# Second block's mixer: splits of queries and keys and the spread of the mLSTM's maxima moved into the projection, gates in pieces, the mLSTM's end pulled apart

## The reference

```
def hybrid_mixer(h, w_in, gate_bias, g_q, g_k, g_mh, w_out):
    proj = (h @ w_in)                       # 1024 -> 3088 columns
    mq, mk, mv, mo, mg, aq, ak, av = split(proj)
    gates = mg.reshape(B, S, 4, 4).transpose(2, 0, 3, 1) + gate_bias
    hm = bidirectional_mlstm(mq, mk * 64 ** -0.5, mv,
             gates[0], log_sigmoid(gates[1]), gates[2], log_sigmoid(gates[3]))
    hm = rms_norm(hm, g_mh) * sigmoid(mo)                  # 4 heads of 128
    qa = partial_rope(rms_norm(aq, g_q), pos) * 64 ** -0.5 # 8 heads of 64
    ka = partial_rope(rms_norm(ak, g_k), pos)
    ha = dilated_attention(qa, ka, av)      # windows 128, 512, 2048; dilations 1, 4, 16
    return concatenate([hm, ha]) @ w_out

mlstm, one direction, per head:  b = cumsum(log_f);  m_t = running maximum
    s = exp(b_t - b_s + li_s - m_t) * (q_t . k_s)  for s <= t
    h = (s @ v) / max(|sum_s s|, exp(-m_t))
```

## Time and profile before

| | us |
|---|---|
| median of three runs | 3399.1 |
| the profiled execution's own time | 3399.85 |
| its span on the core | 3397.7 |
| PE busy in the span | 3129.7 (92%) |
| DVE busy | 1918.7 (56%) |
| ACT busy | 1025.8 (30%) |
| mean granted TensorE clock | 0.947 of full |
| stage of the change: projection, first matmul | 2596.13 |
| side by side, first matmul | 2775.28 |
| output projection, first matmul | 2960.96 |

### The profile page before, as it was taken

The page is one execution under the profiler, slowest core; times in us unless marked ns, Lnnn a source line. Parts: engine busy times, 40 slices in busy tenths (PEclk is TensorE's granted clock), DMA queues, the critical chain, the costliest instruction groups (busy, mean ns, idle before and its releaser), DMA issues.

```text
span 3397.7 us, 36171 instructions
## 1 busy us (share of the span) xinstructions
PE 3129.7 (92%) x14590; PEld 2494.5 (73%) x14590; DVE 1918.7 (56%) x2716; ACT 1025.8 (30%) x1472; POOL 30.3 (1%) x32
## 2 busy tenths in 40 slices
PE   4999999898889999899978999899997989799998
PEld 3788888786667888788865788678886754377886
DVE  6876555635555544566656554566665555554344
ACT  2322222335443222322222222332224245332222
POOL 2000000000000000000000000000000000000000
PEclk6999999898989999999988999899998989699999
DMA  5443333110023433256521443235552200122221
GB/s 189 130 136 131 112 112 106 48 62 10 2 93 127 171 126 109 95 172 216 179 95 61 144 155 124 75 113 192 185 173 70 82 33 1 42 90 98 99 93 51
DMA packets 101905, 365.33 MB, mean 108 GB/s; under 512 B 11230, under 2 KB 12526, under 8 KB 101484
## 3 DMA queue, kind: packets, MB, share of 16 engines
q1 hardware_dynamic: 97644, 351.65, 30.8%
q10 hardware_dynamic: 2944, 6.29, 0.5%
q0 software_dynamic: 1152, 5.07, 0.5%
HBM read 360.87 MB, written 2.10 MB: 107 GB/s over the span
## 4 chain that ended last, share of the span: by engine, by line
PE 84%; DVE 10%; ACT 4%; issue 1%; DMA 1%; ACTq 0%; DVEq 0%; SPq 0%
PE ps L191 24%; PE ps L193 23%; PE ps L192 23%; PE ps L195 4%; PE ps L196 2%; DVE WL L183 1%; DVE DUMP L304 1%; DMA STG<-in_w_modt 1%; ACT WH L178 1%; PE ps L507 1%; DVE RAW L1301 1%; PE ps L2607 0%; DVE XT L815 0%; DVE SQ L575 0%; PE ps L483 0%
## 5 line engine op out<-in xcount | busy, mean ns | idle before, releaser
L191 PE MATMUL ps<-HH,WH 128*128 128x512 f32 x2464 | 980.4, 398 | 34.2 <-DVE HL L564 27.9
L192 PE MATMUL ps<-HL,WH 128*128 128x512 f32 x2464 | 969.3, 393 | 0.0
L193 PE MATMUL ps<-HH,WL 128*128 128x512 f32 x2464 | 968.9, 393 | 0.0
L178 ACT ACTIVATE WH<-RAW 128x1024 fp32r<-128x1024 f32 x456 | 456.6, 1047 | 554.8 <-PE ps L193 409.4
L183 DVE TENSOR_TENSOR WL<-RAW,WH 128x1024 fp32r<-128x1024 f32 x456 | 538.4, 1220 | 103.6 <-ACT WH L178 103.4
L191 PEld LDWEIGHTS ps<-HH,WH 128*128 128x128 f32 x2464 | 468.7, 190 | 144.6 <-issue 42.2
L192 PEld LDWEIGHTS ps<-HL,WH 128*128 128x128 f32 x2464 | 468.6, 190 | 100.2 <-issue 3.8
L193 PEld LDWEIGHTS ps<-HH,WL 128*128 128x128 f32 x2464 | 468.0, 190 | 101.0
L815 DVE SCALAR_TENSOR_TENSOR XT<-ps,DER,XT 128x512 f32<-128x512 f32 x512 | 342.7, 682 | 272.7 <-PE ps L193 258.1
L191 PE MATMUL ps<-GH,WH 128*128 128x512 f32 x1056 | 414.5, 392 | 19.1 <-DVE XT L815 14.3
L192 PE MATMUL ps<-GL,WH 128*128 128x512 f32 x1056 | 412.1, 390 | 0.0
(11 more groups left out here) (358 smaller groups left out, 2409.7 us busy)
## 6 DMA issues: line engine op xcount, KB each, us to landing
RAW<-in_w_modt SPq DMA_DIRECT2D x200, 512.0 KB, 4.5
RAW<-in_ffn_wi SPq DMA_DIRECT2D x176, 512.0 KB, 4.5
RAW<-in_ffn_wo SPq DMA_DIRECT2D x88, 512.0 KB, 4.8
RAW<-in_w_gu SPq DMA_DIRECT2D x88, 512.0 KB, 4.4
RAW<-in_w_in SPq DMA_DIRECT2D x44, 512.0 KB, 3.7
RAW<-in_w_down SPq DMA_DIRECT2D x44, 512.0 KB, 4.5
RAW<-in_w_out SPq DMA_DIRECT2D x16, 512.0 KB, 4.8
MU<-in_w_mod SPq DMA_DIRECT2D x8, 384.0 KB, 8.0
```

Source lines behind the costliest of these rows:

```text
L178: act.e.activation(u.hi, u.ld.view, ACT.Copy).then_inc(u.hi_done.sem, 1)
L191: pe.e.matmul(out, wh, x[0], start=first, stop=False)
L192: pe.e.matmul(out, wh, x[1], start=False, stop=False)
L193: m = pe.e.matmul(out, wl, x[0], start=False, stop=last)
```

## The change

It does the following.

- The ring of weights shrinks from five places to three ahead of the projection (`Ring.shrink`), and the two freed places hold MB, now written during the projection; NUM and MD take the three kept places later. The RAW slots for weights go from six to two ahead of the projection, not behind it, since QH and KH lie in the other four.
- The splits of the attention's queries and keys become a fourth piece behind the rope (`normed_rope`) in the projection. `Begin` waits for the last one.
- `MlTables` moves from `mlstm` into the projection, to where MG is evacuated; SELF, SEL, MKD and other small tiles share memory. The gates' evacuation is two ACT copies of 36 rows instead of four of 4 (columns of the weights and of the bias are put in another order). `MlScan` becomes `MlCum` (cumulative sums), `MlMax` (maxima) and `MlFloor` (the exponential, first thing in `mlstm`).
- `MlBroadcast` is made for one head and direction, eight pieces in the projection, one per chunk, over a side bank (there are four side banks now, 4 to 7, for three).
- The order of chunks is another one: DQ and DV first, MG third, DK and MV taking turns, the four MO last.
- `mlstm`'s pieces: a unit pair (two of the 16 units) takes three pieces instead of four; behind `MlDen` there are three rounds; each `MlSquare` comes two pieces behind its `MlQuot`; behind `MlNewton` there are four rounds. `extra=4` is gone.

```
-                    self.add(MlScan(m))
+                    self.add(MlCum(m))
                     yield
+                    self.add(MlMax(m))
                     yield
                     self.add(MlTurnU(m, pr))
+                    m.mgsplit = self.add(HiLo(self, m.MG, m.MGH[:, :], m.MGL[:, :], [m.max]))
+                    for h in range(4):
+                        for d in range(2):
+                            yield
+                            self.add(MlBroadcast(m, pr, h, d))
...
-                rest = list(range(DV, NIN2)) + list(range(MQ, MG))
-                order = [MG]
-                for i in range(8):
-                    order += [DQ + i] + rest[2 * i:2 * i + 2]
+                order = [DQ, DV, MG, DV + 1, DQ + 1, DV + 2, DV + 3, DQ + 2, MQ, MQ + 1, DQ + 3, MK, MK + 1]
+                for i in range(4):
+                    order += [DK + i, MV + i]
+                order += list(range(MO, MG))
...
-            self.add(Begin([self.group, self.roped, self.turned, self.evacd] + lent))
+            self.add(Begin([self.group, self.turned, self.evacd, ksplit[3].done]))
...
-            self.side_by_side(self.dilated(w, CF, cf, DQt, DKt), self.mlstm(m, mix, a["w_out_2"]), extra=4)
+            self.side_by_side(self.dilated(w, CF, cf), self.mlstm(m, mix, a["w_out_2"]))
...
-        for h in range(4):
-            self.add(MlBroadcast(m, h))
-            yield
         before = None
         for h in range(4):
             self.add(MlMask(m, h))
             for j in range(4):
                 x = self.add(MlExp(m, h, j))
-                yield
+                if j % 2:
+                    yield
                 if before:
                     self.add(MlSum(m, before))
                 self.add(MlProd(m, x))
                 before = x
                 yield
         last = self.add(MlSum(m, before))
-        yield
         self.add(MlDen(m, last.done))
         m.rsplit = self.add(HiLo(self, m.B, m.RH[:, :], m.RL[:, :], [m.inverse]))
-        yield
-        yield
+        for _ in range(3):
+            yield
+        before = None
         for h in range(4):
             quot = self.add(MlQuot(m, h))
             yield
-            self.add(MlSquare(m, h, quot))
+            if before:
+                self.add(MlSquare(m, h - 1, before))
+            before = quot
+            yield
+        self.add(MlSquare(m, 3, before))
         self.add(MlNewton(m))
```

More of the change, by code:

```diff
@@ L145, in __init__ @@
     def __init__(self, P, ld, ring):
-        n = ring.n
+        at = ring.places[ring.n % len(ring.places)]
         ring.n += 1
-        at = n % ring.size
         self.ld = ld
@@ L157, with __init__, shrink @@
 class Ring:
-    def __init__(self, WH, WL, size):
-        self.WH, self.WL, self.size, self.n, self.at = WH, WL, size, 0, {}
+    def __init__(self, WH, WL, places):
+        self.WH, self.WL, self.places, self.n, self.at = WH, WL, list(places), 0, {}
+    def shrink(self, n):
+        size = len(self.places)
+        order = [self.places[(self.n - 2 + i) % size] for i in range(size)]
+        self.places, self.n = order[:n], 2
+        return order[n:], [self.at[at].used for at in order[n:]]
 class Split(Step):
@@ L2094, in scalar @@
         m, t = self.m, self.t
+        act.wait_ge(*m.sel)
         act.wait_ge(*self.ready)
@@ L2100, in scalar, with direction @@
         act.e.activation(m.EM, m.EM, ACT.Ln, bias=1.0).then_inc(t[2].sem, 1)
-class MlScan(Step):
+def direction(x, d):
+    x = x[32 * d:32 * d + 4, :]
+    return x if d == 0 else x[:, ::-1]
+class MlCum(Step):
     def __init__(self, m):
         self.m = m
-        self.t = [m.P.s["ml_dve"].next() for _ in range(7)]
-        self.em = m.P.s["ml_act"].next()
-        m.scan = self
-    @staticmethod
-    def rows(x, d):
-        x = x[32 * d:32 * d + 4, :]
-        return x if d == 0 else x[:, ::-1]
+        self.t = [m.P.s["ml_dve"].next() for _ in range(4)]
+        m.u = self.t[3]
     def vector(self, dve):
-        m, t, rows = self.m, self.t, self.rows
+        m, t = self.m, self.t
         dve.wait_ge(*m.gates)
@@ L2128, in vector, with __init__ @@
         dve.e.tensor_tensor(m.U, m.U, m.B, ALU.subtract).then_inc(t[3].sem, 1)
-        dve.wait_ge(*t[3])
-        for d in range(2):
-            u = rows(m.U, d)
-            dve.e.tensor_tensor_scan(rows(m.MG, d), u, u, -BIG, ALU.max, ALU.max).then_inc(t[4 + d].sem, 1)
-        dve.wait_ge(*t[5])
-        dve.e.tensor_tensor(m.EM, m.B, m.MG, ALU.add).then_inc(t[6].sem, 1)
+class MlMax(Step):
+    def __init__(self, m):
+        self.m = m
+        self.t = [m.P.s["ml_dve"].next() for _ in range(3)]
+        m.max = self.t[2]
+    def vector(self, dve):
+        m, t = self.m, self.t
+        dve.wait_ge(*m.u)
+        for d in range(2):
+            u = direction(m.U, d)
+            dve.e.tensor_tensor_scan(direction(m.MG, d), u, u, -BIG, ALU.max, ALU.max).then_inc(t[d].sem, 1)
+        dve.wait_ge(*t[1])
+        dve.e.tensor_tensor(m.EM, m.B, m.MG, ALU.add).then_inc(t[2].sem, 1)
+class MlFloor(Step):
+    def __init__(self, m):
+        self.m = m
+        m.em = m.P.s["ml_act"].next()
     def scalar(self, act):
         m = self.m
-        act.wait_ge(*self.t[6])
-        act.e.activation(m.EM, m.EM, ACT.Exp, scale=-1.0).then_inc(self.em.sem, 1)
+        act.wait_ge(*m.max)
+        act.e.activation(m.EM, m.EM, ACT.Exp, scale=-1.0).then_inc(m.em.sem, 1)
 class MlTurnU(Step):
     def __init__(self, m, pr):
-        self.m, self.ready = m, m.scan.t[3]
+        self.m, self.ready = m, m.u
         self.b, self.free = pr.sidebank()
@@ L2213 @@
+        act.wait_ge(*self.spread)
+        for t in m.lent:
+            act.wait_ge(*t)
+        act.e.activation(m.MB[self.d * 4 + self.h], m.P.banks[self.b], ACT.Copy).then_inc(self.done.sem, 1)
 class MlMask(Step):
@@ L2736, in __init__ @@
         WL = self.sb(ctx, "WL", [128, NUNIT, 1024], F32R)
-        self.ring = Ring(WH, WL, NUNIT)
+        self.ring = Ring(WH, WL, range(NUNIT))
         self.SQ = self.sb(ctx, "SQ", [128, 2, W], F32)
@@ L3283, in evac @@
                     elif ch == MG:
-                        o, rows = VOFF["gate_bias_2"], (slice(0, 4), slice(32, 36))
-                        self.follow(lag, gates(out([G[rows[g // 2], g % 2, :] for g in range(4)], ACT.Identity, after=[zeroed],
-                                                   bias=[self.VT[rows[g // 2], o + g:o + g + 1] for g in range(4)])))
+                        o = VOFF["gate_bias_2"]
+                        self.follow(lag, gates(out([G[0:36, g, :] for g in range(2)], ACT.Identity, after=after,
+                                                   bias=[self.VT[0:36, o + g:o + g + 1] for g in range(2)])))
+                    elif ch < DK:
+                        i = ch - DQ
+                        self.follow(lag, normed_rope(DQt, QH, QL, i, GQ8[:, 0:1], out(DQt[:, i, :]), qsplit))
```

201 lines of the change are left out of this document (99 added, 102 removed), and 2 rows, old and new, of the table VEC.

## The result

The changed kernel takes 3382.3 us (median of 5 runs, 3380.65 to 3386.26), the kernel before 3399.4 on the same chip. The ratio is 0.995 with an interval of 0.9936 to 0.9965: faster by 17 us. The forecast was 3378 with a range of 3364 to 3391; the time lies in the range, 4 us above the forecast. The profiled execution took 3382.3 us with a span of 3380.5.

A forecast was written before the change was run, and what follows sets the result against it. PE was taken as the bound, losing time where it idles or runs at half clock. Projection, transition, middle and end brought the output projection to 2939 to 2940 from 2960.96: -21 us, so 3378 us, range 3364 to 3391.

The forecast's parts named there:

- Start of the projection: First chunks of the projection: with the new queues the eighth chunk starts near 2645.9 instead of 2657.1, -11 us.
- PE runs short of weights by about 1.4 us: Behind the fourth chunk, near 2624: gates, evacuation and weight split on ACT make PE wait about 1.4 us for weights.
- Spread of the maxima: Rest of the projection: eight broadcasts of two matmuls at 0.23 us, with gaps, add 4 us to a full PE.
- Transition: Projection to first scores: shorter idle gives -4 us, scores at full clock with the exponential's table loaded give -1.5 us.
- The middle: From the scores of q=3 to the mLSTM's last sum: 68 us, ending near 2861 for 2887.7 before.
- The end: From the last sum to the output projection: 78 us, so 2939 to 2940 for 2960.96 before.
- Squares no longer awaited: Attention units q=11 to q=13: PE no longer waits for the mLSTM's squares, so each takes 8.5 to 9 us.
- 12.8 us "as before": From the scores of q=15 to the output projection: the earlier kernel's 12.8 us (2948.15 to 2960.96) taken over unchanged.
- A: Rival for the end: six attention units take 7 us each with PE at full clock, 3366; chance 0.13.
- B: Rival for the end: it stays at half clock and costs 9 to 11 us more, 3388; chance 0.17.
- C: Rival: nothing gained, the borrowed lead is paid back and half of terms lost to late weights, 3396; chance 0.09.
- D: Rival in the projection: with two slots the weights' loads come late, slower, 3422 at 11 us per load; chance 0.04.

The follow-up runs named there:

- e10: The changed kernel with the gates' activations, cumulative sums and maxima in one piece behind the fourth chunk, not three pieces a chunk apart: 3390.1 us.
- e5: The changed kernel with the split of the mLSTM's half of MIX one round later and that of the output weights two rounds later: 3379.6 us.
- e6: The changed kernel with squares moved, the steps of MlDen and MlNewton spread over rounds, and MIX split by chunk: 3359.1 us.

## Why the prediction was right

**Start of the projection, -11 us: right in kind, 5 too small.** The eighth chunk starts 46.5 us behind the first matmul; the forecast had 49.8, before it was 60.8 (2656.88, where the prediction had worked out 2657.1). The 1.4 us for the square of DQ are 0.67, the 1.4 us short of weights behind the gates and the 0.3 behind the sums don't occur. The step that failed is "PE runs short of weights by about 1.4 us": the gates stand on ACT from 2619.7 to 2624.2, and the low part that was held up (2625.78) still came in time. The 18 chunks behind then took 117.9 us with 6.6 of broadcasts, 111.3 without, for 113. So the term was -16. The run with the gates whole (e10) shows that 8 of it hang on the three chunks between the gates and the turning of U.

**Spread of the maxima, +4 us: +6.6.** The count was right, the price per pair of matmuls was not: I took two dense matmuls of 0.23 with small gaps. The starts in the changed kernel's trace and the last dense matmul of the run with the block agree on 0.8. In a block behind the projection they leave 0.8 us from q=3 on; the rest by which that kernel is faster, 3.6 us by the medians, lies at the end and goes with the clock.

**Transition, -4 and -1.5 us: right.** From the last dense matmul (2759.84) to the scores are 1.3 us. Summed, -16 + 6.6 - 4.2 is the lead of 13.7 at q=0, forecast as 11; from q=0 to q=1 5.8 us for 6.8 before, where 5.3 was forecast.

**The middle, 68 us from q=3 to the end of the last sum: 66.** PE has no wait there and full clock; the 5 us put down for `DilQuot` and idle were too many (the four terms as written add up to 67). From q=1 to q=3 it took 21.5 us for the 23.5 forecast. The errors in the start, from q=1 to q=3 and here, 2 to 3 us each, bring the last sum 6 us earlier than forecast; the lead there is 33, not 26.

**The end, 78 us: 89, the step that failed.** From the end of the last sum (2854.25), forecast and measured: to the scores of q=10 9.6 and 8.6; q=10 to q=13 26.5 and 33.2; q=13 to q=14 20 and 18.7; q=14 to q=15 9 and 7.5; from there to the output projection 12.8 and 21.1. Both blocks were priced right. Two statements were wrong. "Squares no longer awaited" looked at when a square's data is ready and not at what stands ahead of it on ACT: in that order it is behind the exponentials of q=11, of q=12 and of q=13. The sign that the prediction named, no idle over 2 us ahead of L2447, failed with it (4.13 and 2.62). The run with the squares moved gives 10 us back. And 12.8 us "as before" took over a stretch whose content had changed: before, `MixSplit` and the weight split were ahead of the count of q=14, now they and the last outputs are beside q=15. It took over the clock as well. This is the stretch from the scores of q=15 to the output projection, before and after:

```profile
2948.14:2960.96 12.82, 8.20 (x78) 5.18 (x76) 7.69 (x16) 5.18 (x10) 0.00 (x0) 0.98 0.54 205
2922.24:2943.32 21.08, 15.77 (x82) 9.89 (x81) 13.87 (x25) 7.32 (x13) 0.00 (x0) 0.55 0.35 124
```

PE stands still for 4.6 and 5.3 us, so 7.6 of the 8.3 us are busy time. Its work is the same but for the spread of two outputs' factors (L2479 and L2480, 2.3 us); the other 5.3 us are the same matmuls at a clock of 0.55 for 0.98. When the splits go later (e5), 3.6 us come back by another way, as idle time: PE is then busy 15.9 of 17.5 us, still at 0.55.

**The rivals.** A (the end flows, 3366) did not happen: the clock is 0.63 to 0.70. With the queues put right it is nearly so, 3359 to 3353. B (half clock, 3388) came nearer than its chance of 0.17: the clock was 0.70 and 0.63, and the end took 11 us more than forecast, where B had 9 to 11; the units from q=10 to q=13 took 11.1 us each, where B had 11.6. Its total wasn't reached because the last sum came 6 us early. Its cause is half of the story: the squares' waits, which B did not have, are worth 10 us when they go, and the clock 5 us between kernels with the same queues there. The two are not independent, since the clock rises when waits go (0.75 with the squares moved, 0.84 in e6). The Trainium skill (TensorE: Matmul & The Clock Gate, section "A second HAM failure mode: psum-queue depth-cycling") tells of such a throttled stretch by short idles, and the windows agree on the clock. C (nothing gained) is excluded by the median; its mechanism, a borrowed lead paid back, did take 15.8 us. D (late weights) did not occur: no matmul of the projection waits for a weight split. The table loads, too, came as the earlier trace rows had it: at 2620.31 a load of 1.28 us and the activation at 2621.60, with nothing between, in the changed kernel; the Trainium skill (ScalarE: Activation LUTs, section "What ACT_TABLE_LOAD costs") adds a drain of about 1.38 us that this trace doesn't show either.

So the total was met within 4 us by a start and middle that were 6 us better and an end that was 11 worse. The kind of gain and its place were forecast rightly; that the number fits so well is luck, since two errors of opposite sign met.

## What to carry to other kernels

When two chains share engines that work in order, price an operation by what stands in front of it in its own queue, not by when its data is ready; an operation that waits for a fresh result of the other chain is the worst neighbour. Put the consumer of a long result (here a high part behind a reciprocal) behind the other chain's short copies: three more `yield` in two places were worth 15 us, the higher clock that followed included, nearly as much as the whole change. And a stretch whose content has been changed must not be taken over "as before", neither its work nor its clock.

## What was not expected

- A matmul on 4 rows between matmuls on 128 costs about 0.33 us, a pair of them 0.83 in all, where the dense step is 0.23; two on rows 0 to 3 and 32 to 35 next to each other start together (four broadcasts, eight matmuls, in 1.42 us).
- Two kernels with the same queues from q=10 on needed 80.4 and 75.2 us for them, at a clock of 0.66 and 0.75. Fillers raised it to 0.85, and with their 13 us of added matmuls the median stayed.
- Nearly the same layout of pieces is worth -1 to -3 us in one kernel and +5 to +8 in another.
